# One bank order for both halves of an output projection, rearranged first loads, and moved steps of attention, splits and convolution in a two-block transformer kernel

## What is computed

```python
def first_block(x, p, ...):
    h = x
    h = h + 0.5 * _rmsnorm(_swiglu(_rmsnorm(h, ffn1_pre_g), w_gate, w_up, w_down), ffn1_post_g)
    h = h + _rmsnorm(_token_mixer(_rmsnorm(h, mix_pre_g), ...), mix_post_g)
    h = h + 0.5 * _rmsnorm(_swiglu(_rmsnorm(h, ffn2_pre_g), ...), ffn2_post_g)
    return h + _rmsnorm(sigmoid(_rmsnorm(h, ple_pre_g) @ ple_w_gate) * (p @ ple_w_proj), ple_post_g)

def second_block(x, p, ...):
    u = _rmsnorm_2(x, norm_mix) @ w_in           # a_b, a_c, a_h, a_z, n_q, ..., n_g, n_z, d_q, ..., d_z
    y_a = a_b * _short_conv(a_c * a_h, conv_w, conv_b) * silu(a_z)
    y_b = _nsa(n_q, ..., gates=sigmoid(n_g), ...) * silu(n_z)
    y_c = _dilated_mixer(d_q, d_k, d_v) * silu(d_z)
    h = x + concatenate([y_a, y_b, y_c]) @ w_out
    h = h + sigmoid(h @ w_ple_gate) * (p @ w_ple_proj)
    return _rmsnorm_2(h, norm_final)
```

## Time and profile before

| | |
|---|---|
| median of 3 runs | 1608.2 us (1607.19 to 1609.42) |
| profiled execution | 1607.8 us, span 1606.1 us |
| PE busy | 1579.2 us (98%) |
| PE weight loads busy | 1284.5 us (80%) |
| DVE busy | 745.8 us (46%) |
| ACT busy | 586.6 us (37%) |
| POOL busy | 170.5 us (11%) |
| mean granted PE clock | 0.997 |
| transfers | 144.61 MB, mean 90 GB/s |

### The profile page before, as it was taken

How to read it: one execution, slowest core, us unless ns; L and a number is a source line. 1 busy time by engine, 2 the same in 40 slices (tenths; PEclk the granted TensorE clock), 3 DMA queues, 4 the chain that set the end, 5 groups by cost and what they waited for, 6 DMA issues and landing times.

```text
span 1606.1 us, 19183 instructions
## 1 busy us (share of the span) xinstructions
PE 1579.2 (98%) x7902; PEld 1284.5 (80%) x7902; DVE 745.8 (46%) x1099; ACT 586.6 (37%) x932; POOL 170.5 (11%) x169
## 2 busy tenths in 40 slices
PE   7999999999999999999999999999999999999998
PEld 6778888888888777888888888888878776777787
DVE  5444223446545443444744323443663555566454
ACT  4323223236432233334522222323672432444333
POOL 2311001101013400110111000110111000001100
PEclk9999999999999999999999999999999999999999
DMA  4432333323332322333233233332225321211331
GB/s 144 133 93 92 104 93 94 103 92 92 92 90 82 104 79 79 93 113 97 79 92 104 94 93 104 92 98 86 95 83 125 83 53 41 53 44 50 96 101 66
DMA packets 123608, 144.61 MB, mean 90 GB/s; under 512 B 18769, under 2 KB 86497, under 8 KB 123521
## 3 DMA queue, kind: packets, MB, share of 16 engines
q1 hardware_dynamic: 122096, 138.57, 28.7%
q0 software_dynamic: 1424, 4.82, 1.2%
HBM read 141.26 MB, written 2.10 MB: 89 GB/s over the span
## 4 chain that ended last, share of the span: by engine, by line
PE 93%; DVE 3%; ACT 1%; issue 1%; DMA 1%; SPq 0%; DVEq 0%; ACTq 0%
PE G L57 86%; PE X L57 5%; PE X L60 2%; PE G L60 1%; DVE h L69 1%; DVE wlo L69 0%; DMA f<-in_x_dram 0%; DVE tmp_t L69 0%; DVE xl L72 0%; DMA raw<-in_w_in_dram 0%; DVE f L69 0%; ACT sq_t L63 0%; ACT whi L63 0%; ACT xh L63 0%; DVE h L72 0%
## 5 line engine op out<-in xcount | busy, mean ns | idle before, releaser
L69 DVE TENSOR_TENSOR wlo<-raw,whi 128x1024 fp32r<-128x1024 f32 (+2 forms) x261 | 315.2, 1216 | 505.1 <-ACT whi L63 504.7
L57 PE MATMUL G<-xh,whi 128*128 128x512 f32 (+1 forms) x1256 | 496.5, 395 | 5.9 <-DVE act_t L69 3.0
L57 PE MATMUL G<-xl,whi 128*128 128x512 f32 (+1 forms) x1256 | 487.1, 388 | 0.8 <-DVE xl L72 0.8
L57 PE MATMUL G<-xh,wlo 128*128 128x512 f32 (+1 forms) x1256 | 486.3, 387 | 0.0
L63 ACT ACTIVATE whi<-raw 128x1024 fp32r<-128x1024 f32 (+2 forms) x261 | 268.3, 1038 | 471.4 <-DMA raw<-in_ffn_w_up_dram 152.4
L57 PEld LDWEIGHTS G<-xh,whi 128*128 128x128 f32 x1256 | 236.2, 188 | 58.7 <-issue 9.5
L57 PEld LDWEIGHTS G<-xl,whi 128*128 128x128 f32 x1256 | 236.1, 188 | 49.9 <-DVE xl L72 1.2
L57 PEld LDWEIGHTS G<-xh,wlo 128*128 128x128 f32 x1256 | 236.4, 188 | 44.4
L69 POOL TENSOR_TENSOR tmp_t<-tmp_t,act_t 128x512 f32<-128x512 f32 x52 | 72.5, 1397 | 590.7 <-DVE tmp_t L69 470.4
L57 PE MATMUL G<-whi,ah 128*128 128x512 f32 x320 | 124.6, 389 | 0.0
L57 PE MATMUL G<-whi,al 128*128 128x512 f32 x320 | 124.5, 389 | 0.0
(11 more groups left out here) (237 smaller groups left out, 1723.0 us busy)
## 6 DMA issues: line engine op xcount, KB each, us to landing
raw<-in_w_in_dram SPq DMA_DIRECT2D x55, 512.0 KB, 3.7
raw<-in_ffn_w_gate_dram SPq DMA_DIRECT2D x88, 256.0 KB, 2.8
raw<-in_ffn_w_up_dram SPq DMA_DIRECT2D x88, 256.0 KB, 3.1
raw<-in_ffn_w_down_dram SPq DMA_DIRECT2D x44, 512.0 KB, 3.7
raw<-in_w_in_dram SPq DMA_DIRECT2D x12, 384.0 KB, 3.2
raw<-in_w_out_a_dram SPq DMA_DIRECT2D x8, 512.0 KB, 3.8
raw<-in_w_out_b_dram SPq DMA_DIRECT2D x8, 512.0 KB, 3.7
raw<-in_w_o_dram SPq DMA_DIRECT2D x8, 512.0 KB, 3.8
```

The lines of the kernel that those rows point to most:

```text
L57: return self.e.matmul(out, lhs, rhs, start=start, stop=stop) if self.e else Idle()
L69: return self.e.tensor_tensor(*a) if self.e else Idle()
```

## The change

- `OUT2_ORDER` is (1, 2, 3, 0) for both halves; DVE's adds of the next bank stand ahead of the low part of the one before.
- Start: PE gets 2, 4 and 10 products of `ident` with itself into `G[3]` (`fill`) between its first steps; ACT splits the first unit after its first operand tile and the second after the fourth; DVE in the same order; tiles 4 and 5 are turned after the second bank of the first unit instead of the first.
- The first feed-forward block pumps after bank position 1 instead of 3, on PE, DVE and GpSimd.
- At p4, ACT scales all 1024 columns of a block and DVE none.
- `compress` has one empty step more at its end; `finish` is one step later.
- vg: bank 0 is evicted and the fourth pump done before the last `ahead`.
- Column tiles: `ahead(n)` stands ahead of the third pump instead of the first; the convolution of h tile m is spread over the four pumps of z tile m.

```diff
@@ -335,7 +335,7 @@
...
-        OUT2_ORDER = ((1, 2, 3, 0), (0, 1, 2, 3))
+        OUT2_ORDER = ((1, 2, 3, 0), (1, 2, 3, 0))
@@ -515,7 +515,7 @@
...
                     for k in (2 * b, 2 * b + 1):
                         for i in (2 * half, 2 * half + 1):
-                            pe.wait_ge(normed_dve if b > 1 else normed_act, (st, i))
+                            pe.wait_ge(normed_dve if b > 1 and st != "p4" else normed_act, (st, i))
                             t = pe.transpose(X[b][:, (k % 2) * 256 + (i % 2) * 128:(k % 2) * 256 + (i % 2) * 128 + 128],
@@ -610,21 +610,30 @@
...
+            def fill(n):
+                for _ in range(n):
+                    pe.matmul(G[3][:, 0:128], ident[:, :], ident[:, :], True, True)
+
             pe.wait_ge(const, "ident")
+            fill(2)
             pe.wait_ge(g_in, "g")
             pe.transpose(X[2][:, 0:8], rows[0:8, :], ident[0:8, 0:8]).then_inc(*prep_mm.event("g"))
-            for k in range(4):
-                turn(k)
+            fill(4)
+            turn(0)
+            turn(1)
+            fill(10)
+            turn(2)
+            turn(3)
 
             def rest():
                 turn(6)
                 turn(7)
 
             hooks = pre_hooks("s0")
-            hooks[0, 0] = lambda: (turn(4), turn(5))
+            hooks[0, 1] = lambda: (turn(4), turn(5))
             hooks[2, 1] = rest
             background.append(prepare())
-            ffn("ffn1", XT["x0"], "p1", hooks, (3,))
+            ffn("ffn1", XT["x0"], "p1", hooks, (1,))
@@ -880,6 +889,7 @@
                             if i == 3 and r_ == 2:
                                 t.then_inc(*cmp_done.event(("s", g)))
                 yield
+                yield
...
             def norm_f(st, i):
 
                 act.wait_ge(r_done, (st, i))
-                act.activation(ft(i, 0), ft(i, 0), ACT.Copy, scale=rpost[:, i:i + 1]).then_inc(*normed_act.event((st, i)))
+                of = ftok[:, i, :] if st == "p4" else ft(i, 0)
+                act.activation(of, of, ACT.Copy, scale=rpost[:, i:i + 1]).then_inc(*normed_act.event((st, i)))
@@ -1160,10 +1171,12 @@
                 cross(post, pre, gain, head, factor)
 
 
-            for k in range(4):
-                start_hi(k)
-                if k in (1, 3):
-                    split_hi()
+            start_hi(0)
+            split_hi()
+            start_hi(1)
+            start_hi(2)
+            start_hi(3)
+            split_hi()
@@ -1431,14 +1445,18 @@
...
-            along(("vg",), 4, ahead, background, (1,), {(6, 0): lambda: take_vg(0)})
+            along(("vg",), 4, ahead, background, (1,), leave=1)
+            take_vg(0)
+            pump(background)
             for i in range(1, 4):
                 take_vg(i)
+            ahead(plan["vg",][0] + 3)
             act.wait_ge(scaled, ("vg", 3))
             sigmoid_exp(gates[:, :, :], gates[:, :, :], "gates")
             for name, m, n in tiles_in:
-                ahead(n)
                 for k in range(1, KD, 2):
+                    if k == 5:
+                        ahead(n)
                     pump(background)
@@ -1543,6 +1561,8 @@
 
             def norm_f(st, i):
 
+                if st == "p4":
+                    return
                 dve.wait_ge(r_done, (st, i))
                 dve.tensor_scalar(ft(i, 1), ft(i, 1), rpost[:, i:i + 1], None, ALU.mult).then_inc(*normed_dve.event((st, i)))
@@ -1700,12 +1720,14 @@
             dve.wait_ge(prep_mm, "g")
             dve.tensor_copy(cols[:, 0:8], X[2][:, 0:8]).then_inc(*scaled.event("g"))
             dve.wait_ge(scaled, "g")
-            for k in range(4):
-                turn(k)
-                if k:
-                    start_lo(k - 1)
-                if k == 2:
-                    split_lo()
+            turn(0)
+            turn(1)
+            start_lo(0)
+            split_lo()
+            start_lo(1)
+            turn(2)
+            turn(3)
+            start_lo(2)
             start_lo(3)
             split_lo()
@@ -1728,7 +1750,7 @@
...
-            ffn("ffn1", "s0", "p1", "s1", (lambda m: half[:, m:m + 1], "mix_pre_g"), ("v", 0), hooks, (3,))
+            ffn("ffn1", "s0", "p1", "s1", (lambda m: half[:, m:m + 1], "mix_pre_g"), ("v", 0), hooks, (1,))
@@ -2017,8 +2040,8 @@
                         operand(AT["o"], 2 + r_, tmps[2])
 
                 score(DIL)
+                yield
                 finish()
-                yield
                 score(DIL + 1)
                 scale(DIL)
                 yield
@@ -2044,14 +2067,39 @@
...
-            along(("vg",), 4, ahead, background, (1,), {(6, 0): lambda: take_gates(0)})
+            along(("vg",), 4, ahead, background, (1,), leave=1)
+            take_gates(0)
+            pump(background)
             for i in range(1, 4):
                 take_gates(i)
+            ahead(plan["vg",][0] + 3)
             sigmoid_of(gates[:, :, :], "gates")
...
+            def conv(m, step):
+
+                s, u, cv = acts[2 * m], cac[:, m, :], ccv[:, m, :]
+                w = [cols[:, colat["conv_w_2"] + 2 * k + m:colat["conv_w_2"] + 2 * k + m + 1] for k in range(3)]
+                if step == 0:
+                    dve.wait_ge(stored, ("h", m))
+                    dve.tensor_tensor(u, s, u, ALU.mult).then_inc(*mixed.event(("conv", m, 0)))
+                elif step == 1:
+                    dve.wait_ge(mixed, ("conv", m, 0))
+                    dve.tensor_scalar(cv, u, w[2], col("conv_b_2", m), ALU.mult, ALU.add).then_inc(*mixed.event(("conv", m, 1)))
+                elif step == 2:
+                    dve.wait_ge(mixed, ("conv", m, 1))
+                    dve.scalar_tensor_tensor(cv[:, 1:], u[:, :T - 1], w[1], cv[:, 1:], ALU.mult,
+                                             ALU.add).then_inc(*mixed.event(("conv", m, 2)))
+                else:
+                    dve.wait_ge(mixed, ("conv", m, 2))
+                    dve.scalar_tensor_tensor(cv[:, 2:], u[:, :T - 2], w[0], cv[:, 2:], ALU.mult,
+                                             ALU.add).then_inc(*mixed.event(("conv", m, 3)))
+
             for t_no, (name, m, n) in enumerate(tiles_in):
-                ahead(n)
                 for k in range(1, KD, 2):
+                    if name == "z":
+                        conv(m, k // 2)
+                    if k == 5:
+                        ahead(n)
                     pump(background)
@@ -2068,19 +2116,7 @@
...
                 elif name == "h":
-                    s, u, cv = acts[2 * m], cac[:, m, :], ccv[:, m, :]
...
-                    store(s)
-                    dve.wait_ge(stored, (name, m))
-                    dve.tensor_tensor(u, s, u, ALU.mult).then_inc(*mixed.event(("conv", m, 0)))
...
-                    dve.tensor_scalar(cv, u, w[2], col("conv_b_2", m), ALU.mult, ALU.add).then_inc(*mixed.event(("conv", m, 1)))
...
-                    dve.scalar_tensor_tensor(cv[:, 1:], u[:, :T - 1], w[1], cv[:, 1:], ALU.mult,
...
-                    dve.scalar_tensor_tensor(cv[:, 2:], u[:, :T - 2], w[0], cv[:, 2:], ALU.mult,
-                                             ALU.add).then_inc(*mixed.event(("conv", m, 3)))
+                    store(acts[2 * m])
                 elif name == "z":
                     store(acts[1 + 2 * m])
                 else:
@@ -2097,11 +2133,21 @@
...
             for c in range(2):
                 along(("out2", c), 4, ahead, background, (3,) if c else ())
-                for m in OUT2_ORDER[c]:
+
+                def onto(m):
                     j = 4 * c + m
                     dve.wait_ge(acc_done, (("out2", c), m))
                     dve.tensor_tensor(hs[j], G[m][:, :], hs[j], ALU.add).then_inc(*h_done.event(("x5", j)))
-                    operand(XT["x5"], j, hs[j])
+
+                m0, m1, m2, m3 = OUT2_ORDER[c]
+                onto(m0)
+                onto(m1)
+                operand(XT["x5"], 4 * c + m0, hs[4 * c + m0])
+                onto(m2)
+                operand(XT["x5"], 4 * c + m1, hs[4 * c + m1])
+                onto(m3)
+                operand(XT["x5"], 4 * c + m2, hs[4 * c + m2])
+                operand(XT["x5"], 4 * c + m3, hs[4 * c + m3])
             drain(background)
@@ -2226,7 +2272,7 @@
...
-            ffn("ffn1", (3,), {(2, 1): first_squares})
+            ffn("ffn1", (1,), {(2, 1): first_squares})
```

5 lines of the change are left out of this document (removed).

## The result

The changed kernel takes 1592.05 us (median of four runs, 1589.68 to 1593.23) where the kernel before takes 1608.81 beside it (1607.19 to 1609.95): ratio 0.9895, 95% interval 0.9878 to 0.9912. Of the six executions behind 1591.31 one took 4916.09 us and one 1597.43, and the other four lie between 1591.07 and 1591.42. The profiled execution took 1592.56 us, span 1590.8, against 1607.8 and 1606.1: 15.3 us less in span, where the sum said 12.4.

A forecast was written before the change was run, and what follows sets the result against it. TensorE was taken as the bound, so only removing its pauses or low-clock stretches helps. Terms -2.3 - 2.4 + 0.2 - 0.9 - 3.2 - 3.8 = -12.4 from 1607.8, plus 0.4 for the median: 1595.8 us, range 1592.5 to 1600.0.

The forecast's parts named there:

- First loads and fills: Kernel start: fills and earlier first split bring the first matmul to 11.7 at full speed; gain 2.3 us (0.4 to 4.0).
- So it moves along: Start: GpSimd's sum of squares, hanging on tiles 6 and 7, would end earlier by the same 2.3 us.
- Pumps: First feed-forward block: preparation steps after the second bank remove two group-start waits, 1.32 and 1.07; gain 2.4 us.
- vg: vg projection: evicting bank 0 before the split removes PE's 0.93 wait for gates; gain 0.9 us, at least 0.5.
- Boundary: Fourth block boundary p4: ACT's longer whole-row scaling outweighs DVE's dropped half rows; 0.2 us slower (-0.4 to +0.8).
- Attention: Attention: the empty step, later splits and spread convolution remove five PE waits totalling 3.49; gain 3.2 us (0.5 to 3.5).
- 0.3 was left at the copies: Attention's coarse chain: a new 0.3 us wait kept at ACT's copies, since ACT's split stands directly ahead.
- Output projection: Output projection: one bank order gains 4.6 at half 1, new ple-gate wait 0.8 to 1.0; net gain 3.8 us.
- R1: Start: clock stays low through the fills, first matmul 13.1, gain only 0.4; 1597.7 us; chance 0.16.
- R2: Attention: waits return one step later beside store and convolution, gaining 0.5 instead of 3.2; 1598.5 us; chance 0.14.
- R3: Start and boundary reach their good ends, gaining 4.0 and 0.4; 1593.5 us; chance 0.07.
- R4: Attention: each of 24 sparse steps waits 0.71 on DVE's or ACT's queue; 1616.0 us, slower; chance 0.03.

The follow-up runs named there:

- u_three: Changed kernel with first feed-forward pumps at 3, vg's old order and each output-projection add followed by its own subtraction put back; 1602.03 us.
- after_again: The changed kernel run once more, unaltered; median 1591.31 us, ratio 0.9905 to the kernel before.
- after_more: The changed kernel unaltered, run again on another occasion for a direct comparison on one chip; median 1592.70 us, ratio 0.9901 to the kernel before.
- a_both: Changed kernel with both attention edits undone (empty step and the splits' place), convolution still spread; 1595.10 us.
- b_order: Kernel before with one edit, the output projection's second half in bank order 1, 2, 3, 0; 1605.81 us (before on that chip 1608.6).
- s_nofill: Changed kernel with all sixteen fill products left out; 1593.93 us.
- s_six: Changed kernel with the first six fills kept and the ten behind them left out; 1592.44 us.
- x_best2: Changed kernel plus ple gate's first unit in banks 1, 2, 3, 0, output transposes before last sums, coarse scores' 48 products in two steps; median 1592.64 us.
- a_splitback: Changed kernel with the weight split back at each projection tile's start, empty step and spread convolution kept; 1597.20 us.

## Why the prediction was right in its direction and short by 3 us

Of the 2.9 us between 12.4 and 15.3, the start holds 1.4, the boundary 0.9, attention 0.6, the pumps 0.2; the output projection was 0.2 too high and the tail took 0.1. The rest of the 3.75 us between 1595.8 and the median, 0.9, is the 0.4 put on the profiled time for the median, which did not carry over (the changed kernel's profiled execution is 0.5 above its median), and that 0.5. So three terms of the sum failed: the price of the fills at the start, the path of the boundary, and the cost of a wait in attention. Chance stands beside them: the low clock of the coarse chain (1.6 lost in this profile), and two stops that this profile was spared (below).

**First loads and fills, forecast 2.3, measured 3.74.** Mechanism right, term mis-sized. The failed step is the price of the ten fills: between 4.3 us "at the low level" and "high from about 9" I took a first matmul at 11.7. It came at 10.11: the fills ran at 0.24 each, since the level rose at 5.56 (between 5.05 and 8.21 in the thirteen traces with all the fills), and in this trace they lie wholly in the time in which PE waits for x. (Where the level rose later they took up to 3.10 us, and in six of the thirteen traces PE has no wait for x behind them.) The low price was too small, 0.52 and not 0.43, but was hardly paid. The first unit was through at 16.56, where the second begins, and not at 18.3 (20.72 in the kernel before): a gain of 4.2, past my good end of 4.0. "So it moves along" was wrong too: GpSimd's sum came 3.74 earlier and not 4.18, and 0.4 was given back there. Only u_three, with its rise at 8.21 and its first matmul at 10.97, looked like my forecast (start gain 2.7).

**Pumps, 2.4, measured 2.63** (2.7 by u_three): right, by the steps given. What was missed is the restart: the listed idle time is not all that a wait costs.

**vg, 0.9, measured 0.96.** The wait on the gates is gone, as forecast, but the size is in part luck. The same stretch is 0.40 longer in after_again and 0.67 longer in after_more, so the gain is 0.3 to 1.0 in three traces of one program. In eleven of the fifteen traces with most of the change, u_three among them, PE waits 0.21 to 0.86 for ScalarE's tmp_t near 1251; in the changed kernel's profile it does not. The changed kernel, then after_more:

```profile
1247.48 1.06 ACT L63 ACTIVATE whi<-raw 128x1024 fp32r<-128x1024 f32 x1 [1.69 <-DMA raw<-in_w_in_dram]
...
1250.04 0.37 ACT L63 ACTIVATE tmp_t<-X,stat 128x128 f32<-128x128 f32 x1 [1.50 <-DVE stat L78]
```

```profile
1248.08 1.06 ACT L63 ACTIVATE whi<-raw 128x1024 fp32r<-128x1024 f32 x1 [2.33 <-DMA raw<-in_w_in_dram]
...
1250.64 0.37 ACT L63 ACTIVATE tmp_t<-X,stat 128x128 f32<-128x128 f32 x1 [1.49 <-DVE stat L78]
...
1251.15 1.04 PE L57 MATMUL X<-dk,dq 64*128 64x256 f32 x4 [0.48 <-ACT tmp_t L63]
```

In after_more ScalarE's split, which waits for a weight unit's landing, starts 0.60 later. VectorE's half of the split follows it (1249.17, not 1248.57), the maximum that tmp_t needs stands behind that half on VectorE, and tmp_t comes 0.60 later too. This is read from two traces; no experiment moved that split.

**Boundary, +0.2, measured -0.70.** The sign was wrong. The new wait ahead of the transposes came (0.59, bound 0.8), but I added ScalarE's longer rows to PE's path although the prediction itself said that PE's next wait, 1.42, ends by DVE's queue. Once that was said, the earlier wait was free up to 1.42, and the half rows taken off DVE, 2 x 0.48 ahead of xl at most, were the only term left; 0.73 of it arrived.

**Attention, 3.2, measured 3.84 with 1.6 of low clock in it,** so 5.4 against 3.2. Three things. The five waits of the earlier trace rows sum to 3.49 in idle time, but the shifts at them are 0.85 + 0.34, 1.00, 0.82, 0.33 + 0.27 and 1.06, together 4.67: the product behind a wait also runs longer (0.83 where it takes 0.49 without a wait). Of the 4.67 the two attention edits bring 4.1 by a_both. No 0.3 was left at the copies. And 0.7 is a stop of PE in the w1s products, at 1333.06 in the kernel before, that names no releaser; b_order (0.39), s_nofill and s_six (0.47 each) have it, the other thirteen traces don't, and no trace has both it and the wait on tmp_t. No edit aims at it and its cause is open, so its absence in this profile can't be put down to the change. The split of the credit was wrong too: the wait on sq_t was put to the missing step and belongs to the splits.

**Output projection, 3.8, measured 3.57,** with both halves of the reasoning shown: 4.66 gained at half 1 (forecast 4.6), about 1.0 given back at the gate (0.83 idle), and the 1.9 that the gate would have cost without the adds first.

**The rivals.** R1 did not come, in any trace. R2 did not. R3 was the nearest, 1593.5, and got 0.07; it let only two terms be good. My range summed good ends for hardly more than that, as though the terms' errors would cancel, when they had one direction: I had rounded each unknown against the change. R4's waits on ptr are absent. Its threshold was a slip: with the 3.2 of attention lost, (1608.2 - 1595.8 - 3.2) / 24 = 0.38 us per step would already have reached the kernel before, not 0.65.

## What to carry to other kernels

A wait's cost is the shift of the instructions behind it, idle time plus restart, 0.1 to 0.4 us each here. When two waits of one engine follow each other and the second ends by another engine's queue, price the second's end alone: work ahead of the first is free up to its length, and an instruction taken off that queue is worth up to its duration (0.73 of 2 x 0.48 here). Where a group changes its order, give it the order in which its banks come free, and enter the next group in that order for its first unit alone.

## What the runs showed of the hardware that I had not expected

The same program's clock differs between executions: low for 3.4 us in a narrow-product stretch in five of 11, worth 1.5 to 1.7 us, with PE never idle in it. A pause of PE of 2.7 us was followed by a fall in two traces of three (the kernel before and u_three, not b_order), one of 2.55 in x_best2 was not, one of 1.96 in a_splitback was. The Trainium skill, "TensorE: Matmul & The Clock Gate", Part 1: The HAM clock gate, says that the number of slow matmuls at a kernel's start varies from run to run; the first rises here agree, and the same held in the middle of the program. The level's first rise came 5.05 to 8.21 us into the span with the fills, and at 13.57 without them (16.36 in the kernel before, 15.60 in b_order, which has its start). Output stores of 2.1 MB took the place of the evictions as the end of the program as soon as these came 5 us earlier.
